# Ten of the odd layer's modulation runs moved from TensorE to GpSimd, beside the even layer's feed-forward

## The chip, the cores and the metric

The kernel runs on one core of a Trainium2 chip. The metric is the device time of one execution in microseconds (us). The core has five engines that run beside each other and meet at semaphores: TensorE (PE, matrix products into the PSUM banks), VectorE (DVE), ScalarE (ACT), GpSimd (POOL, which can't reach PSUM) and SyncE (SP), whose queue issues nearly all DMA loads.

## The reference, cut to what matters

A block with a mixture of experts is followed by two transformer layers over 256 tokens of width 1024. Both are modulated by one vector `c`:

```python
cond = jax.nn.silu(c)                                   # 1 x 1024
for l in range(2):
    mod = cond @ ada_w[l] + ada_b[l]                    # 1 x 6144
    sh1, sc1, g1, sh2, sc2, g2 = split(mod, 6)
    h = rms_norm(x, norm_mix[l]) * (1 + sc1) + sh1
    y = even_mixer(h) if l % 2 == 0 else odd_mixer(h)
    x = x + g1 * (y @ w_out[l])
    h = rms_norm(x, norm_ffn[l]) * (1 + sc2) + sh2
    x = x + g2 * ((silu(h @ wg) * (h @ wu)) @ wd)       # hidden width 2816
```

All data are float32. The change concerns `cond @ ada_w[l]`, a product of one row with a 1024 x 6144 matrix, for each layer 12 pieces of 1024 x 512 (2 MB each).

## The kernel before, in words

The tokens' products are made from weights split in a high and a low part. A load of 2 MB is four chunks of 128 x 1024. For each chunk ScalarE copies the high part (`begin`), VectorE subtracts it from the chunk to leave the low part in place (`ring_r<-ring,W_c_r` or `X_c_r`), and TensorE makes the three products of high and low parts: 24 matmuls of 256 columns, or 12 of 512. `Feed(lag=5)` issues `begin` of a chunk five chunks ahead of its use, and six buffers for the high part bound how far ahead that gets.

Loads go through a ring of `NR = 5` slots of 2 MB, in the order of `plan.loads`. SP issues them in that order; before each it waits until the load that had the slot five loads earlier has been used (`freed`, lines 396 to 402, waited for at line 640). A load that waits holds back all behind it.

A piece of the modulation is a **run** and a **close**. The run (`ada` on TensorE, line 1832) makes 8 matmuls of 512 columns with the weights of the piece into bank 7 (`ps[7]`), which leaves 128 partial rows. ScalarE copies the bank to `acc` (`s_acp`). The close multiplies `acc` with ones: for an ordinary piece four small products, which make columns that VectorE adds to the bias into `modc` (`s_modc`); for the last two pieces of the odd layer (`row_gate`) two products of 512 columns that make a row spread over all partitions, which ScalarE copies to `gates` (`s_gate`). Bank 7 and `acc` exist once, so runs and closes take turns; the next run waits until the bank is read out. `cs` holds silu(c)/32, and `csr` is `cs` repeated 32 times for the run.

The order of work is written by `Plan`: `ada(point)` puts the close of the piece before and a new run at a point of the program. Points are `("u", n, u)`, just after the scores of unit u of attention n; `("f", i)`, at `begin` of chunk i; `("n", l, which)`, inside a modulation (`modulated`), after the squares; and `("o", j)`, ahead of an output projection. Each engine walks the same points. Pieces 0 to 11 are of the even layer and 12 to 23 of the odd one. Pieces 12 and 13 run in the even layer's attention, 14 at the even feed-forward's modulation, 15 in its down projection, 16 at the odd layer's first modulation, and 17 to 23 in the odd attention, one in each second unit up to unit 12.

The stages in which the change works are, in order: output projection of the even mixer, `ffn(0)` (a modulation, 11 loads of gate and up weights, 6 loads of down weights), the odd layer's first modulation, its projections `kvo`, `q0`, `q1`, the odd attention of 16 units (`attend(4, ...)`), output projection, `ffn(1)`. A modulation (`modulated`) adds the gated result to `x` on VectorE, squares on ScalarE, sums on TensorE, makes the reciprocal root on VectorE in eight small operations (`root_parts`, line 1202), spreads it with TensorE, and then gives eight slices of the input in high and low part (`scaled` and `rest`, line 1363). TensorE's products of the next stage wait for these slices.

Side work, like head norms, is stepped between these by `side.go`. GpSimd makes masks and constants at the start and selects in the even layer's index search; after `attend(3, 2)` it has nothing to do.

Of the kernel before, what the change touches and what calls it, by code (L numbers as in the profile page):

```python
# [9 lines left out]
ALU = mybir.AluOpType  # L10
# [10 lines left out]
class Chain:  # L21
# [3 lines left out]
    def __init__(self, e, own):  # L25
        self.e, self.own, self.n, self.last = e, own, {}, None
# [50 lines left out]
class Feed:  # L77
# [30 lines left out]
    def product(self, i0, n, then):  # L108
        self.then[i0 + n - 1] = then
        for i in range(i0, i0 + n):  # L110
            self(i)
# [9 lines left out]
class Plan:  # L121
# [1 line left out]


    def __init__(self):
        self.loads, self.ada_order, self.rows = [], [], {}
        self.chunks, self.first = [], {}
        self.pending = None
        self.moe, self.experts = {}, []
# [13 lines left out]
    def ada(self, point):  # L143
        self.close(point)
        v = self.pending = len(self.ada_order)
        self.ada_order.append((v // 12, v % 12, self.load("ada", v // 12, v % 12)))
        self.rows.setdefault(point, []).append((v, "run"))

    def product(self, name, n, part=None):
        k = self.load("w", name)  # L150
# [19 lines left out]
            if u == wo_at:  # L170
                self.out_loads(j)

    def ffn(self, l, turn_run, run):
        self.first["gu", l] = len(self.chunks)
        for u in range(11):
            k = self.load("gu", l, u)
            for q in (0, 2, 1, 3) if u == 0 else range(4):
                self.feed(k, q)
            if u == 0 and turn_run:
                self.ada(("n", l, 3))  # L180
        self.first["dn", l] = len(self.chunks)
        for u in range(6):
            k = self.load("w", ("dn", l, u))
            for q in range(min(4, 22 - 4 * u)):
                if run is not None and 4 * u + q == run:
                    self.ada(("f", len(self.chunks)))
                if run is not None and 4 * u + q == run + 3:
                    self.close(("f", len(self.chunks)))
                self.feed(k, q)


def make_plan():
    p = Plan()
    for name in ("gqk", "mqk", "mkv"):
        p.product(name, 4)
    for name in ("mvq", "gv", "gr"):
        p.product(name, 4)
    p.units(1, 8, (0, 2, 4, 6), 2, 0)
    p.close(("o", 0))
    p.out_proj(0)  # L200
    for g in range(NX // 4):
        for name in ("w_gate", "w_up", "w_down"):
            for q in range(4):
                p.experts.append(p.load("moe", name, g, q))
    k = p.load("w", "ak")
    p.first["ak"] = len(p.chunks)
    for q in range(3):
        p.feed(k, q)
    p.ada(("n", 0, 0))
    p.feed(k, 3)  # L210
    for name in ("aq", "av", "kvi"):
        p.product(name, 4)
    p.product("tli", 2)
    p.ada(("f", len(p.chunks)))
    p.product("bq", 4)
    p.close(("f", len(p.chunks) - 1))
    p.units(2, 8, (0, 2, 4, 6))
    p.units(3, 8, (0, 2, 4, 6), 2, 1)
    p.close(("o", 1))
    p.out_proj(1)  # L220
    p.ffn(0, True, 6)
    k = p.load("w", "kvo")
    p.first["kvo"] = len(p.chunks)
    for q in range(4):
        p.feed(k, q)
    p.ada(("n", 1, 0))
    p.product("q0", 4)
    p.product("q1", 4)
    p.units(4, 16, (0, 2, 4, 6, 8, 10, 12), 8, 2)
    p.close(("o", 2))  # L230
    p.out_proj(2)
    p.ffn(1, False, None)
    p.end = len(p.chunks)
    return p


def build(nc, A, out_ap, dbg):
    ctx = ExitStack()
    with ctx:
        part = [ctx]  # L240

        def sb(name, shape, dt=FP):
            return part[0].enter_context(nc.sbuf_tensor(name, shape, dt))

        def both(name, shape):
            with nc.sbuf_tensor(name + "_r", shape, FR) as rounded:
                pass
            return sb(name, shape), rounded
# [6 lines left out]
        def sem(name):  # L255
            return ctx.enter_context(nc.semaphore(name))
# [3 lines left out]
        ring, ringR = both("ring", [128, NR, 4096])  # L260
# [19 lines left out]
        modc = sb("modc", [128, 2, 6, 8])  # L280
        gates = sb("gates", [128, 1024])
        cs = sb("cs", [128, 8])
        acc = sb("acc", [128, 512])
        csr = sb("csr", [128, 8, 32])
        qcol = sb("qcol", [128, 18])
# [70 lines left out]
        s_rowx, s_cs, s_ar, s_acp, s_ac, s_gate, s_modc = [sem("s_ada_" + n) for n in ("row_exp", "cs", "run", "copied", "closed", "gate", "col")]  # L356
# [19 lines left out]
        plan = make_plan()  # L376
        nload = len(plan.loads)
        m0, m1_ = plan.experts[0], plan.experts[-1]
        order, slot, before = list(range(NR)), [], {}
# [11 lines left out]
        landed, used = [], [0] * (NR + MR)  # L391
# [4 lines left out]
        freed = {}  # L396
        for i, (k, q) in enumerate(plan.chunks):
            freed[k] = (s_use, i + 1)
        for v, (_, _, k) in enumerate(plan.ada_order):
            freed[k] = (s_ar, v + 1)  # L400
        for m, k in enumerate(plan.experts):
            freed[k] = (s_mm, m + 1)

# [317 lines left out]
        def gpsimd(pool):  # L721
            G = Chain(pool, s_pool)
# [20 lines left out]
            def attend(n, beside):  # L743
                for u in range(len(attns[n].units)):
                    side.go(beside)
                    if n == 3 and u == 4:
                        side.until(ev, "sel1")
# [38 lines left out]
            side.until(ev, "sel0", "bT")  # L786
            attend(3, 2)
            side.end()

# [382 lines left out]
        def vector(dve):  # L1174
# [567 lines left out]
            def ffn(l, n):  # L1742
# [29 lines left out]
                feed.drain()  # L1772

            ffn(0, 1)


# [786 lines left out]
```

## Time and profile before

| what | value |
|---|---|
| device time, median of 3 runs | 1473.1 us (1470.25 to 1476.48) |
| the profiled execution's own time | 1468.73 us |
| its span, first to last instruction | 1467.0 us |
| mean granted clock of TensorE | 0.880 of full speed |
| TensorE, VectorE, ScalarE, GpSimd busy | 1191.2, 615.8, 475.6, 7.6 us |
| read from memory | 366.28 MB, 250 GB/s over the span |

The profile is of one execution. A page gives busy times, the chain of work that ended last and the costliest groups of instructions. Timelines give the start and the length of instructions in us, and in brackets the idle time ahead of one and who ended it. `csr` marks a run, `ones,acc` the close of an ordinary piece, `acc,ones` and `gates,ones` the close of a row piece. All operations of VectorE, ScalarE and GpSimd that go through the helper `Chain` have line L32, all matmuls line L1826 and all transposes line L1830, so tiles tell them apart. The granted clock is given as a part of 2.4 GHz.

### The profile page before, as it was taken

What the parts mean: (1) busy time and instruction counts of PE and PEld (TensorE: products, weight loads), DVE (VectorE), ACT (ScalarE), POOL (GpSimd) and SP (SyncE); (2) the same over time, 40 slices, a digit from 0 to 9 for tenths busy, and PEclk for the clock granted to TensorE, in tenths of its full rate; (3) what the DMA queues carried; (4) which work ended last, traced back from release to release, by engine and by line L of the source; (5) the groups of instructions that cost most, each with busy time, mean ns of one, the idle gap of its engine ahead of it and who ended that gap; (6) DMA issues with size and microseconds to landing.
All of it is one profiled execution on the core that took longest, in us unless ns stands there. A gap on an engine that the chain in (4) does not pass through costs nothing.

```text
span 1467.0 us, 19464 instructions
## 1 busy us (share of the span) xinstructions
PE 1191.2 (81%) x7703; PEld 874.9 (60%) x7703; DVE 615.8 (42%) x1240; ACT 475.6 (32%) x767; POOL 7.6 (1%) x54
## 2 busy tenths in 40 slices
PE   5888888575676756846897888999999978999998
PEld 4665565242332323413675438899898735999986
DVE  3473652010010000101663676655535656565553
ACT  4561621000000000002532335555433447455541
POOL 1000000000000000000000000000000000000000
PEclk9897888798888878978897678899999988999999
DMA  8542149999999999999446431865546472655520
GB/s 294 173 150 80 59 168 424 430 429 430 431 429 428 431 430 428 431 425 401 164 152 244 172 116 58 264 204 203 191 151 223 174 274 70 222 181 187 205 98 29
DMA packets 121729, 368.67 MB, mean 251 GB/s; under 512 B 9842, under 2 KB 56093, under 8 KB 110878
## 3 DMA queue, kind: packets, MB, share of 16 engines
q1 hardware_dynamic: 120556, 367.26, 65.1%
q8 instruction: 64, 1.05, 0.3%
q10 hardware_dynamic: 1074, 0.08, 0.1%
q14 instruction: 35, 0.29, 0.1%
HBM read 366.28 MB, written 1.05 MB: 250 GB/s over the span
## 4 chain that ended last, share of the span: by engine, by line
PE 57%; DMA 22%; DVE 12%; ACT 5%; issue 3%; SPq 1%; DVEq 0%; ACTq 0%
PE ps L1826 54%; DMA more<-in_w_gate_dram 8%; DMA more<-in_w_down_dram 7%; DMA more<-in_w_up_dram 6%; PE ps L1830 3%; DVE st L32 3%; DVE ring_r L32 2%; DVE R_c L32 2%; SPq L669 1%; DVE X_c L32 1%; DVE R_a L32 1%; DVE X_a L32 1%; ACT W_c_r L32 1%; ACT X_c L32 1%; DVE sc L32 1%
## 5 line engine op out<-in xcount | busy, mean ns | idle before, releaser
L1826 PE MATMUL ps<-hT_r,ring_r 128*128 128x256 f32 x864 | 243.7, 282 | 0.0
L1826 PE MATMUL ps<-ring,xg 128*32 128x512 f32 x640 | 140.1, 734 | 126.1 <-DMA more<-in_w_gate_dram 79.3
L1826 PEld LDWEIGHTS ps<-ring,xg 128*32 128x32 f32 x640 | 36.9, 132 | 222.3 <-issue 222.3
L1826 PEld LDWEIGHTS ps<-hT_r,ring_r 128*128 128x128 f32 x864 | 166.0, 192 | 0.0
L32 DVE TENSOR_TENSOR ring_r<-ring,W_c_r 128x1024 fp32r<-128x1024 f32 x94 | 115.2, 1225 | 96.3 <-ACT W_c_r L32 92.4
L1826 PE MATMUL ps<-R_c_r,W_c_r 128*128 128x256 f32 x608 | 152.7, 283 | 0.0
L32 DVE TENSOR_TENSOR ring_r<-ring,X_c_r 128x1024 fp32r<-128x1024 f32 x88 | 107.8, 1225 | 95.2 <-ACT X_c_r L32 92.3
L1826 PE MATMUL ps<-R_c_r,X_c_r 128*128 128x256 f32 x576 | 147.7, 284 | 0.0
L1826 PE MATMUL ps<-more,xg 128*32 128x512 f32 x384 | 134.6, 726 | 0.0
L32 ACT ACTIVATE W_c_r<-ring 128x1024 fp32r<-128x1024 f32 x94 | 99.7, 1060 | 87.3 <-PE ps L1826 83.0
L32 ACT ACTIVATE X_c_r<-ring 128x1024 fp32r<-128x1024 f32 x88 | 93.3, 1061 | 89.6 <-PE ps L1826 84.4
L32 DVE TENSOR_TENSOR x<-x,ps 128x512 f32<-128x512 f32 x36 | 24.8, 688 | 231.3 <-PE ps L1826 231.0
L1826 PE MATMUL ps<-hT_r,X_c_r 128*128 128x256 f32 x416 | 118.3, 284 | 2.9 <-DVE R_c_r L32 2.5
L1826 PE MATMUL ps<-hT_r,W_c_r 128*128 128x256 f32 x416 | 118.6, 285 | 1.9 <-DVE R_c_r L32 1.8
L1826 PEld LDWEIGHTS ps<-R_c_r,W_c_r 128*128 128x128 f32 x608 | 108.8, 190 | 0.0
L1826 PEld LDWEIGHTS ps<-R_c_r,X_c_r 128*128 128x128 f32 x576 | 104.0, 191 | 1.5 <-issue 1.5
L1826 PE MATMUL ps<-ring_r,hT_r 128*128 128x512 f32 (+1 forms) x240 | 94.8, 395 | 0.0
L1826 PEld LDWEIGHTS ps<-hT_r,X_c_r 128*128 128x128 f32 x416 | 78.8, 189 | 4.4 <-issue 3.0
L1826 PEld LDWEIGHTS ps<-hT_r,W_c_r 128*128 128x128 f32 x416 | 79.7, 191 | 2.7 <-DVE R_c_r L32 2.2
L1826 PE MATMUL ps<-ring,csr 128*32 128x512 f32 x384 | 63.6, 794 | 13.1 <-DVE modc L32 12.6
L1826 PE MATMUL ps<-ring,hid 128*32 128x512 f32 x320 | 60.2, 654 | 12.7 <-DMA more<-in_w_down_dram 11.6
L1826 PE MATMUL ps<-sel,hn 128*128 128x128 f32 x256 | 63.1, 410 | 2.1 <-DVE sel L32 2.1
(280 smaller groups left out, 1912.4 us busy)
## 6 DMA issues: line engine op xcount, KB each, us to landing
ring<-in_ada_w_dram SPq DMA_DIRECT2D x24, 2048.0 KB, 8.1
ring<-in_w_gate_dram SPq DMA_DIRECT2D x20, 2048.0 KB, 18.9
ring<-in_w_up_dram SPq DMA_DIRECT2D x20, 2048.0 KB, 20.0
ring<-in_w_down_dram SPq DMA_DIRECT2D x20, 2048.0 KB, 19.4
more<-in_w_gate_dram SPq DMA_DIRECT2D x12, 2048.0 KB, 27.9
more<-in_w_up_dram SPq DMA_DIRECT2D x12, 2048.0 KB, 28.4
more<-in_w_down_dram SPq DMA_DIRECT2D x12, 2048.0 KB, 27.9
ring<-in_ffn_gate_dram SPq DMA_DIRECT2D x22, 1024.0 KB, 5.9
```

What stands on the lines that cost most here:

```text
L32: op(*args, **kw).then_inc(sem, 1)
L669: sp.dma_start(dst, src).then_inc(s_w[slot[k]], 16)
L1826: return pe.matmul(out, lhsT, rhs, start=start, stop=stop, skip_group_check=True)
L1830: return pe.transpose(out, in_, ident[0:n, 0:n])
```

## The change

Pieces 14 to 23 no longer run on TensorE. GpSimd scales each of the 8 weight slices of a piece with its column of `cs32` (silu(c)), in place in the ring's slot, and adds it to `acc`: 8 `tensor_scalar` and 7 `tensor_tensor` instructions of 128 x 512, each waiting for the one before. The last raises `s_acp`, which frees the slot and lets TensorE close the piece as before. Each GpSimd run waits for its load and for the close of the piece before (`s_ac`). The loads stand behind gate-up loads 0, 2, 4, 6, 8 and 10, behind down loads 1 and 3, behind the last down load, and behind `kvo`. A close stands at `begin` of the chunk three before the next pooled load; the eighth at the first chunk of `kvo`, the ninth (first row gate) at the first of `q1`, and the last at unit 0 of the odd attention. In steady state closes are eight chunks apart. No run is left in the odd attention, and the two loads of its output projection come right behind `q1`.

```diff
@@ class Plan @@
+    def pool_run(self, shift=-3):
+        self.close(("f", len(self.chunks) + shift))
+        v = self.pending = len(self.ada_order)
+        self.ada_order.append((v // 12, v % 12, self.load("ada", v // 12, v % 12)))
+        self.pooled.append(v)
...
-    def ffn(self, l, turn_run, run):
+    def ffn(self, l, gate_up_runs=(), down_runs=()):
...
-            if u == 0 and turn_run:
-                self.ada(("n", l, 3))
+            if u in gate_up_runs:
+                self.pool_run()
...
-                if run is not None and 4 * u + q == run:
-                    self.ada(("f", len(self.chunks)))
-                if run is not None and 4 * u + q == run + 3:
-                    self.close(("f", len(self.chunks)))
                 self.feed(k, q)
+            if u in down_runs:
+                self.pool_run()
@@ def make_plan @@
-    p.ffn(0, True, 6)
+    p.ffn(0, (0, 2, 4, 6, 8, 10), (1, 3))
+    p.pool_run(0)
...
-    p.ada(("n", 1, 0))
+    p.pool_run(4)
     p.product("q0", 4)
     p.product("q1", 4)
-    p.units(4, 16, (0, 2, 4, 6, 8, 10, 12), 8, 2)
-    p.close(("o", 2))
+    p.out_loads(2)
+    p.close(("u", 4, 0))
     p.out_proj(2)
-    p.ffn(1, False, None)
+    p.ffn(1)
@@ def build @@
+        cs32 = sb("cs32", [128, 8])
...
-            freed[k] = (s_ar, v + 1)
+            freed[k] = (s_acp if v in plan.pooled else s_ar, v + 1)
@@ def gpsimd, at its end @@
+            pool.wait_ge(s_cs, 1)
+            G(pool.tensor_scalar, cs32[:, :], cs[:, :], 32.0, None, ALU.mult)
+            for v in plan.pooled:
+                k = plan.ada_order[v][2]
+                w = ring[:, slot[k], :].rearrange("p (c n) -> p c n", c=8)
+                pool.wait_ge(*landed[k])
+                pool.wait_ge(s_ac, v)
+                G(pool.tensor_scalar, acc[:, :], w[:, 0, :], cs32[:, 0:1], None, ALU.mult)
+                for c in range(1, 8):
+                    G(pool.tensor_scalar, w[:, c, :], w[:, c, :], cs32[:, c:c + 1], None, ALU.mult)
+                    G(pool.tensor_tensor, acc[:, :], acc[:, :], w[:, c, :], ALU.add, up=s_acp if c == 7 else None)
```

## Rows read from the trace of the kernel before

**Rows 1.** The page: the span, and each engine's busy us, share and instructions.
```profile
span 1467.0 us, 19464 instructions
...
PE 1191.2 (81%) x7703; PEld 874.9 (60%) x7703; DVE 615.8 (42%) x1240; ACT 475.6 (32%) x767; POOL 7.6 (1%) x54
```

**Rows 2.** Windows: stretch, length, busy us of each engine, granted clock, DMA share, GB/s.
```profile
940.00:1055.00 115.00, 115.00 (x979) 115.00 (x978) 67.81 (x73) 59.42 (x73) 0.00 (x0) 1.00 0.61 202
1146.00:1158.00 12.00, 12.00 (x53) 9.76 (x53) 10.35 (x21) 6.37 (x8) 0.00 (x0) 1.00 0.81 291
1172.00:1195.00 23.00, 15.24 (x85) 7.05 (x83) 10.58 (x37) 8.11 (x19) 0.00 (x0) 0.70 0.53 188
1195.00:1207.00 12.00, 12.00 (x106) 6.81 (x105) 8.40 (x34) 8.49 (x25) 0.00 (x0) 1.00 1.02 377
1226.00:1233.00 7.00, 4.31 (x40) 2.50 (x36) 4.35 (x17) 5.87 (x18) 0.00 (x0) 1.00 0.00 0
```

**Rows 3.** The chain in order of time, 920 to 1135 us: start, us, what.
```profile
929.79 125.61 PE ps L1826 x1050
```

**Rows 4.** VectorE's groups by form, 940 to 1055 us.
```profile
L32 DVE TENSOR_TENSOR ring_r<-ring,X_c_r 128x1024 fp32r<-128x1024 f32 x22 | 27.0, 1225 | 19.7 <-ACT X_c_r L32 18.7
...
L32 DVE TENSOR_TENSOR R_c_r<-sc,R_c_r 128x512 fp32r<-128x512 f32 x10 | 6.9, 692 | 1.0
```

**Rows 5.** Timeline of GpSimd: start us, us, line, operation, what it waited for.
```profile
4.16 0.40 POOL L32 TENSOR_SCALAR_AFFINE_SELECT negw<-negd 128x256 f32<-128x256 f32 x1
4.63 0.15 POOL L32 IOTA iotI<- 128x32 int32 x1
...
814.44 0.29 POOL L32 TENSOR_SCALAR_AFFINE_SELECT R_c<-R_c 128x128 f32<-128x128 f32 x1 [709.92 <-DVE R_c L32]
```

**Rows 6.** Timelines of VectorE and TensorE at the first modulation.
```profile
923.90 0.42 DVE L32 SCALAR_TENSOR_TENSOR sc<-st 128x256 f32<-128x256 f32 x1
...
922.22 3.64 PE L1826 MATMUL ps<-ring,csr 128*32 128x512 f32 x16
925.79 1.22 PE L1826 MATMUL ps<-ident,sc 128*128 128x128 f32 x4
```

**Rows 7.** Timeline of TensorE at the start of the even down projection.
```profile
1057.96 0.95 PE L1826 MATMUL ps<-ones,acc 128*128 128x1 f32 x8
1062.29 2.55 PE L1826 MATMUL ps<-ring,csr 128*32 128x512 f32 x16 [3.37 <-DVE modc L32]
```

**Rows 8.** Timeline of TensorE at the odd layer's first modulation.
```profile
1129.83 1.92 PE L1826 MATMUL ps<-ring,csr 128*32 128x512 f32 x16
1131.98 0.71 PE L1826 MATMUL ps<-ident,sc 128*128 128x128 f32 x4 [0.24 <-DVE sc L32]
```

**Rows 9.** Timeline of TensorE at the start of the odd attention.
```profile
1178.87 3.64 PE L1826 MATMUL ps<-ring,csr 128*32 128x512 f32 x16 [5.13 <-DVE modc L32]
...
1189.45 3.64 PE L1826 MATMUL ps<-ring,csr 128*32 128x512 f32 x16
```

**Rows 10.** Timeline of TensorE in the odd attention: two units.
```profile
1195.55 0.49 PE L1826 MATMUL ps<-R_c 64*128 64x128 f32 x4
1195.97 1.92 PE L1826 MATMUL ps<-ring,csr 128*32 128x512 f32 x16
...
1199.19 1.05 PE L1826 MATMUL ps<-ones,acc 128*128 128x1 f32 x8
...
1201.35 0.49 PE L1826 MATMUL ps<-R_c 64*128 64x128 f32 x4
```

**Rows 11.** TensorE's groups by form, 1195 to 1226 us.
```profile
L1826 PE MATMUL ps<-acc,ones 128*128 128x512 f32 x4 | 2.2, 644 | 0.0
L1826 PE MATMUL ps<-gates,ones 1*128 1x512 f32 x4 | 2.2, 640 | 0.0
```

**Rows 12.** Timeline of ScalarE past the last run: the same operation two units apart.
```profile
1227.40 0.51 ACT L32 ACTIVATE X_c<-X_c,s 128x257 f32<-128x257 f32 x1
...
1231.65 0.51 ACT L32 ACTIVATE X_c<-X_c,s 128x257 f32<-128x257 f32 x1
```

More of the change, by code:

```diff
@@ L125, in __init__ @@
     def __init__(self):
-        self.loads, self.ada_order, self.rows = [], [], {}
+        self.loads, self.ada_order, self.rows, self.pooled = [], [], {}, []
         self.chunks, self.first = [], {}
```

## The prediction

> **What bounds the kernel now.** I read the page first, then the windows, then the chain in order of time with the timelines of single stretches. The page [rows 1] shows TensorE busy for 81% of a span of 1467.0 us and GpSimd for 1%; the time around the span is 1.7 us, since the profiled execution took 1468.73 us. The three runs shown have the median 1473.1 us, 4.4 us more: I make the sum against 1468.7 and carry its difference over to 1473.1. The change touches nothing before the even layer's feed-forward, so only 920 to 1240 us matters. The windows [rows 2] show that there TensorE is busy throughout, in the feed-forward (115 of 115 us) and in the odd attention (12 of 12), with VectorE at 59% in the feed-forward and 86% in the odd projections. The chain [rows 3] is TensorE alone for 125.6 us: 1050 matmuls, 0.120 us each, so a chunk of 24 costs 2.87 us. What lengthens TensorE's queue counts in full; what VectorE or ScalarE do counts where TensorE waits for them.
>
> **Part 1: what leaves the odd attention.** Seven runs and seven closes stood in the 16 units. In the steady part two units take 5.80 us (1195.55 to 1201.35), of which the run is 1.92 and the close 1.05 [rows 10]; the last two closes are of the row form and cost 2.2 [rows 11]. Without them TensorE needs 5.80 - 1.92 - 1.05 = 2.8 us for two units, and the next engine sets the pace. That is ScalarE: past the last run it takes 4.25 us for two units, 1227.40 to 1231.65 [rows 12]. Five such pairs, three at 5.8 and two at about 6.9, become 5 x 4.25: 31.3 - 21.3 = 10 us. At the start, the second run waits 5.13 us for VectorE's bank copy and then takes 3.64, and the third takes 3.64 again [rows 9], because the lower level of the clock is granted for much of that stretch (mean 0.70 [rows 2], full being 2.4 GHz and the lower level 1.2). VectorE's head norms stay in that stretch, so of these 12 us I count about 6.5: the second unit's scores need not wait, and the third run stood just before the first turn. Together 16.5 us. Against it: an engine at 2.8 us of work in 4.25 may be granted the lower level, as a run shows it (3.64 against 1.92 [rows 9, 10]); then the pair costs 2.8 x 1.9 = 5.3 rather than 4.25 and the gain is 11. I take 14.
>
> **Part 2: what the even feed-forward gains and loses.** The run in its down half goes: 2.55 us, and with it 3.37 us in which TensorE waited for VectorE to free bank 7 [rows 7]. Five more closes come in (seven rather than two), 0.95 each [rows 7]: 4.75. Net -1.2. They are in front of chunks that TensorE has ready five ahead, so VectorE's copy after each is hidden. The run beside the first modulation (3.64 us) ends at 925.8, and the spreading of the reciprocal root starts only then, while VectorE had it ready at 924.3 [rows 6]: 1.5 us to gain if nothing else is late. The run beside the odd layer's first modulation ended just when VectorE was ready (0.24 us of idle remain [rows 8]): nothing to gain. There a close now stands in front of the squares: +1.0. The close of the first row gate moves into the odd projections, where TensorE has 12.0 of 12 us busy [rows 2]: +2.2 [rows 11]. ScalarE loses ten copies of bank 7, off the chain.
>
> **Part 3: the GpSimd run.** A run is 8 one-input and 7 two-input operations on 128x512, each waiting for the one before. No such row exists. The nearest are the selects: 0.29 us for 128 columns, 0.40 for 256, and 0.47 from one start to the next [rows 5]; 0.11 more per 128 columns gives 0.62 busy and 0.69 start to start at 512. For two inputs the bounds are the same price (0.69) and twice it (1.38); I double the streaming part alone, 0.69 + 0.44 = 1.13. A run is 8 x 0.69 + 7 x 1.13 = 13.4 us, bounds 10.4 and 15.2. The room for it: a run starts when TensorE has closed the one before and must end by the next close, 8 chunks on, 8 x 2.87 = 22.9 us, 23.9 with the close. Alone it fits with 9 us to spare and the whole gain stands. The GPSIMD Engine Reference of the Trainium skill (section 3.1) gives 4497 ns for a two-input add of 2048 columns, an estimate of 1.1 to 1.2 us for 512, so by it the sum stays.
>
> **Part 4: does GpSimd run beside VectorE?** In the trace its selects on real data run only after a wait for VectorE (709.92 us for one [rows 5]), so no row shows both reading. Bounds: full overlap, costing nothing, and no overlap with VectorE's instructions that read two SBUF tensors. Per 8 chunks those are 8 subtractions of 1.225 and 2 of 0.692 [rows 4]: 11.2 us. Full exclusion needs 13.4 + 11.2 = 24.6 us, and about 1.2 for close and semaphores, against 23.9: up to 1.9 us of stall in each of six periods, 11 us. If the 0.25 us of each GpSimd operation that isn't streaming overlaps (15 x 0.25 = 3.8), there is none. I take 5. VectorE's own delays in the feed-forward are covered by its five-chunk lead: it is idle for 47 of 115 us [rows 2]. They are not covered in the two modulations, where TensorE waits for VectorE. Run 22 starts with the close in front of the odd layer's modulation and lasts through it: seven small two-input operations and eight of 0.49 us each can meet a GpSimd operation of 0.6 to 1.05 us. Bounds 0 and 8 us; I take 4. In the first modulation run 14 is well under way (its slot comes free in the middle of the output projection): I put 2.5 us of delay against the 1.5 us gained, +1; bounds -1.5 and +3. In the projections VectorE is at 10.35 of 12 us [rows 2] and run 23 shares it: bounds 0 and 5, I take 2.
> The Trainium skill (SBUF — State Buffer, Who interferes with whom) says that a VectorE instruction with two SBUF inputs and a GpSimd instruction that reads SBUF exclude each other for the whole instruction. By that rule the sum is near the upper ends of these bounds, by plain overlap at the lower ones; no row here decides.
>
> **The queues.** On SP's queue every pooled load keeps its slot until GpSimd's last operation; loads behind it wait in order. The tightest is the gate-up load five loads after a pooled one: its slot comes free at a close, and its chunks are wanted two units (23 us) later. DMA share is 0.61 there [rows 2]; a third load for each two adds about half, under 1. I put nothing on it. If GpSimd is late, TensorE's close waits, and with it all later chunks, VectorE's column copy and GpSimd's next run.
>
> **The sum.** -14 (attention) - 1.2 (closes for the down run) + 1 (first modulation) + 5 (late runs) + 1 + 4 (odd modulation) + 2.2 (row close) + 2 (projections) = 0. So 1468.7 in the profiled execution's terms, **1473 us** beside the median.
>
> **Rivals.**
> *Full overlap, faster.* GpSimd and VectorE don't touch. For it: nothing in the trace speaks against, and VectorE is idle 41% of the feed-forward. Sum: -14 - 1.2 - 1.5 + 1 + 2.2 = -13.5, so 1459.6 us.
> *GpSimd paces the feed-forward, slower.* One mechanism: the run and VectorE's 11.2 us add up beyond the period. It decides from a run over 12.7 us under full exclusion (23.9 - 11.2). At 15.2 a period is 15.2 + 11.2 + 1.2 = 27.6, so 3.7 us of stall, six times: 22 rather than 5. The odd modulation then takes 7 rather than 4 and the projections 5 rather than 2: 1468.7 + 17 + 3 + 3, with the attention at -13, 1492.7; beside the median 1497 us.
> *The clock.* The attention without runs stays at the lower level throughout and hands it to the output projection: its gain is 8 and not 14, 1479 us. Against it: between 1226 and 1233, without runs, where ScalarE sets the pace already, the full level was granted [rows 2].
>
> **How the numbers follow.** My forecast (partial exclusion) has 0.40, full overlap 0.34, GpSimd as the pace 0.20, the clock alone 0.06. The forecast's own range is 1466 to 1481. The range for 8 in 10 leaves out only the outer part of both side cases: 1457 to 1493. Faster by over 0.5% (7.4 us, about what a measurement of this kernel can tell from no change): full overlap nearly whole and a tenth of the forecast, 0.35. Slower: GpSimd's case and a fifth of the forecast, 0.29. Within: 0.36.
>
> **What would show it.** In the new profile: one GpSimd run from first to last operation (13.4 alone, 20 to 24 shared) and whether its operations are longer while VectorE subtracts; TensorE's idle time in front of its ones-by-acc matmuls; VectorE's small operations in the modulation before the odd projections, 0.2 us apart or more; the time for two units (4.25 or 5.3) and the granted clock beside it. The prediction is wrong if GpSimd's operations are far from 0.69 and 1.13, if the two engines overlap wholly, or if the attention has another bound than ScalarE.

## The result, and the profile after

The changed kernel takes 1519.5 us (median of 4 runs, 1514.76 to 1521.33) against 1471.7 for the kernel before on the same chip: ratio 1.0318, interval 1.0278 to 1.0358. It is slower by 3.2%; I had forecast no change, and the time lies far above my range. The profiled execution took 1518.23 us, its span is 1516.5, 49.5 us more than [rows 1].

The page of the changed kernel: the span, busy us of each engine, then tenths of busy time, of the granted clock and of GpSimd in 40 slices.

```profile
span 1516.5 us, 19276 instructions
...
PE 1194.9 (79%) x7543; PEld 894.7 (59%) x7543; DVE 656.6 (43%) x1240; ACT 469.5 (31%) x757; POOL 258.2 (17%) x205
...
PE   5888877566665675667896888888897867999998
...
POOL 1000000000000000000000005899895630000000
PEclk9897888788896897887996578999999787899999
```

TensorE has 160 matmuls less and yet is busy for 1194.9 us, 3.7 more than before; VectorE is busy for 41 us more with as many instructions. Of GpSimd's 258 us, some 250 are in one block; the rest is at the start, as before.

By landmarks in both timelines (first and last product of a stage, first scores) the 49.5 us divide like this:

| stage | before | after | difference |
|---|---|---|---|
| up to the first product of the even feed-forward | 928.8 | 935.8 | +7.0 |
| the even feed-forward, first to last product | 197.6 | 229.5 | +31.9 |
| from there to the first product of `kvo` (odd modulation) | 8.1 | 22.1 | +14.0 |
| projections, to the first scores of the odd attention | 37.8 | 46.8 | +9.0 |
| odd attention, to the first product of its output projection | 67.5 | 54.4 | -13.1 |
| the rest | 227.2 | 227.9 | +0.7 |

**The feed-forward.** Windows of the changed kernel, with the columns of [rows 2]: first the same 115 us as there, then one period from a GpSimd run to the next (950.75 to 980.8), then the last 40 us with a run but without a close in the way, then the odd modulation.

```profile
940.00:1055.00 115.00, 101.54 (x789) 100.99 (x789) 70.33 (x66) 48.03 (x59) 99.24 (x58) 0.91 0.67 220
950.60:980.70 30.10, 24.60 (x201) 24.43 (x202) 21.41 (x19) 14.25 (x18) 26.65 (x15) 0.94 0.85 278
...
1125.70:1166.00 40.30, 40.30 (x344) 40.30 (x343) 13.61 (x11) 12.73 (x12) 25.05 (x15) 1.00 0.75 275
1166.00:1187.00 21.00, 8.31 (x38) 7.87 (x37) 14.41 (x26) 4.18 (x10) 19.62 (x13) 0.56 0.31 113
```

GpSimd is now busy for 99 of 115 us and TensorE for 101.5, with 789 matmuls where it had 979. That period is 30.1 us where I had 23.9; from 950.75 to 1125.8 the six periods are 27.3 to 30.3. Beside a run (1125.7 to 1166) TensorE is as fast as before; only a close that comes too early for GpSimd stops it. The view of TensorE's waits from 935 to 1170 us (us in total, times, the longest), and the timelines of GpSimd and TensorE around one such close:

```profile
PE ps L1846 <- POOL acc L32: 19.9, 6, 5.5
```

```profile
974.91 2.41 POOL L32 TENSOR_SCALAR ring<-ring,cs 128x512 f32<-128x512 f32 x1
977.41 1.26 POOL L32 TENSOR_TENSOR acc<-acc,ring 128x512 f32<-128x512 f32 x1
...
978.81 1.84 PE L1846 MATMUL ps<-ones,acc 128*128 128x1 f32 x8 [5.50 <-POOL acc L32]
980.51 0.56 PE L1846 MATMUL ps<-hT_r,X_c_r 128*128 128x256 f32 x1
980.87 0.41 PE L1846 MATMUL ps<-R_c_r,X_c_r 128*128 128x256 f32 x1
981.09 0.41 PE L1846 MATMUL ps<-hT_r,ring_r 128*128 128x256 f32 x1
```

TensorE waits 5.50 us for the last addition, its close then takes 1.84 us and not 0.95, and the next products have 0.21 us between starts, not 0.12: after the idle time it is granted the lower of its levels, 1.2 in place of 2.4 GHz, for a while (0.89 to 0.94 on average over each of the six periods; 1.00 in 1125.7 to 1166 and in [rows 2]). The waits themselves are 19.9 us; what else the feed-forward lost is products made at this clock, as experiment 1 shows.

**The GpSimd run.** Its first instructions, beside a VectorE that has few subtractions to do, and its groups from 940 to 1120 us, with their means in ns:

```profile
923.08 1.63 POOL L32 TENSOR_SCALAR acc<-ring,cs 128x512 f32<-128x512 f32 x1 [73.70 <-DMA ring<-in_ada_w_dram]
924.80 1.57 POOL L32 TENSOR_SCALAR ring<-ring,cs 128x512 f32<-128x512 f32 x1
926.46 1.27 POOL L32 TENSOR_TENSOR acc<-acc,ring 128x512 f32<-128x512 f32 x1
...
944.91 1.33 POOL L32 TENSOR_TENSOR acc<-acc,ring 128x512 f32<-128x512 f32 x1
```

```profile
L32 POOL TENSOR_SCALAR ring<-ring,cs 128x512 f32<-128x512 f32 x43 | 86.1, 2002 | 4.2
L32 POOL TENSOR_TENSOR acc<-acc,ring 128x512 f32<-128x512 f32 x43 | 62.6, 1456 | 3.6
```

The first run takes 23.2 us (923.08 to 946.24); those in full feed-forward 26 to 28. A scaling is 1.56 us alone and 1.65 from start to start, where I had 0.62 and 0.69; an addition is 1.27 and 1.37, where I had 1.13 from start to start. VectorE's groups over the same stretch as [rows 4]:

```profile
L32 DVE TENSOR_TENSOR ring_r<-ring,X_c_r 128x1024 fp32r<-128x1024 f32 x16 | 24.3, 1518 | 10.6 <-ACT X_c_r L32 9.6
L32 DVE TENSOR_TENSOR R_c_r<-sc,R_c_r 128x512 fp32r<-128x512 f32 x7 | 9.2, 1314 | 0.7
```

1225 and 692 ns have become 1518 and 1314, and GpSimd's operations are longer too: each side waits for the other.

**The odd modulation.** Timelines of VectorE and TensorE from the close of piece 21, at 1165:

```profile
1166.17 0.16 DVE L32 TENSOR_TENSOR modc<-ps,cols 128x4 f32<-128x4 f32 x1 [7.65 <-PE ps L1846]
1166.44 1.62 DVE L32 TENSOR_TENSOR ring_r<-ring,X_c_r 128x1024 fp32r<-128x1024 f32 x1
1168.16 1.55 DVE L32 TENSOR_TENSOR ring_r<-ring,W_c_r 128x1024 fp32r<-128x1024 f32 x1
1169.82 2.12 DVE L32 TENSOR_TENSOR ring_r<-ring,X_c_r 128x1024 fp32r<-128x1024 f32 x1
...
1172.82 2.11 DVE L32 SCALAR_TENSOR_TENSOR x<-ps,modc,x 128x256 f32<-128x256 f32 x4
```

```profile
1165.18 0.95 PE L1846 MATMUL ps<-ones,acc 128*128 128x1 f32 x8
1173.90 6.96 PE L1846 MATMUL ps<-ones,sc 128*128 128x1 f32 x32 [7.76 <-ACT sc L32]
1184.28 1.22 PE L1846 MATMUL ps<-ident,sc 128*128 128x128 f32 x4 [3.43 <-DVE sc L32]
1187.43 0.77 PE L1846 MATMUL ps<-X_c_r,hT_r 128*128 128x512 f32 x1 [1.93 <-DVE R_c_r L32]
```

The close stands at the first chunk of `kvo`, and in VectorE's queue its `modc` addition is ahead of three subtractions, which were done before the feed-forward's end in the kernel before, and of the gated additions to `x`. VectorE idles 7.65 us for a close that TensorE can make only after its last product. Then three subtractions, and only then `x`; ScalarE's squares and TensorE's sums wait, the clock falls, and the sums take 6.96 us, not the 3.63 of the kernel before:

```profile
1126.27 3.63 PE L1826 MATMUL ps<-ones,sc 128*128 128x1 f32 x32
```

GpSimd's timeline beside the first and the third of these subtractions shows how the two engines meet:

```profile
1166.30 1.56 POOL L32 TENSOR_SCALAR acc<-ring,cs 128x512 f32<-128x512 f32 x1 [14.14 <-issue]
...
1169.60 1.26 POOL L32 TENSOR_TENSOR acc<-acc,ring 128x512 f32<-128x512 f32 x1
```

The third subtraction starts inside the addition, which ends at 1170.86, and ends 1.08 us after it: of its 1.23 us nearly all comes behind the addition. The first starts 0.14 us into the scaling, which ends at 1167.86, and ends only 0.20 us after it: it got through while the scaling still ran. So it is all through this trace: the 15 subtractions that start inside an addition, before its last 0.1 us, end 1.07 to 1.09 us after it; the 11 that start 0.14 to 0.35 us into a scaling of 1.56 us end 0.19 to 0.21 us after it. An operation of GpSimd that starts inside a subtraction is done 1.43 to 1.46 us (scaling) or 1.14 to 1.16 us (addition) after the subtraction's end, so it waits for all of it.

**The odd attention.** TensorE's timeline, first and last scores of six pairs of units without runs:

```profile
1247.11 0.80 PE L1846 MATMUL ps<-R_c 64*128 64x128 f32 x4
...
1274.91 0.49 PE L1846 MATMUL ps<-R_c 64*128 64x128 f32 x4
```

27.8 us for six pairs, 4.6 each, against 5.80 [rows 10]: between the 4.25 that I took and the 5.3 of the lower clock, and the granted clock from 1247 to 1286 is 0.74. In these 39 us TensorE is busy for 31.4, VectorE for 30.1 and ScalarE for 27.3; TensorE's waits there end on VectorE (5.6 us, 7 times) and once on ScalarE (1.0).

### The profile page after: what moved, and what is told of

It is laid out like the page before. It is cut to its first block and busy times, and to the rows that moved or that the text cites. A ratio compares the mean times of both kernels' runs of the same rounds, so it can differ in the third digit from the quotient of the medians.

```text
span 1516.5 us, 19276 instructions
## 1 busy us (share of the span) xinstructions
PE 1194.9 (79%) x7543; PEld 894.7 (59%) x7543; DVE 656.6 (43%) x1240; ACT 469.5 (31%) x757; POOL 258.2 (17%) x205
## 5 line engine op out<-in xcount | busy, mean ns | idle before, releaser
L1846 PE MATMUL ps<-hT_r,ring_r 128*128 128x256 f32 x864 | 250.8, 290 | 0.0
L1846 PEld LDWEIGHTS ps<-hT_r,ring_r 128*128 128x128 f32 x864 | 169.5, 196 | 0.0
L32 DVE TENSOR_TENSOR ring_r<-ring,W_c_r 128x1024 fp32r<-128x1024 f32 x94 | 125.9, 1340 | 98.0 <-ACT W_c_r L32 93.6
L32 DVE TENSOR_TENSOR ring_r<-ring,X_c_r 128x1024 fp32r<-128x1024 f32 x88 | 119.4, 1357 | 88.5 <-ACT X_c_r L32 85.0
L32 POOL TENSOR_SCALAR ring<-ring,cs 128x512 f32<-128x512 f32 x70 | 133.6, 1909 | 6.8
L1846 PE MATMUL ps<-hT_r,W_c_r 128*128 128x256 f32 x416 | 122.0, 293 | 2.4 <-DVE R_c_r L32 2.3
L1846 PEld LDWEIGHTS ps<-R_c_r,W_c_r 128*128 128x128 f32 x608 | 114.5, 200 | 0.0
L32 POOL TENSOR_TENSOR acc<-acc,ring 128x512 f32<-128x512 f32 x70 | 99.0, 1414 | 5.8
```

The lines of the kernel that those rows point to most:

```text
L32: op(*args, **kw).then_inc(sem, 1)
L1846: return pe.matmul(out, lhsT, rhs, start=start, stop=stop, skip_group_check=True)
```

## The experiments

Each kernel is timed against the kernel before on its chip. The changed kernel has 1.0318.

### 1. GpSimd's work taken away, its places kept

The changed kernel, in which a run is one operation of 8 columns. It leaves out scaling and adding.

```diff
-                G(pool.tensor_scalar, acc[:, :], w[:, 0, :], cs32[:, 0:1], None, ALU.mult)
-                for c in range(1, 8): ...
+                G(pool.tensor_scalar, acc[:, 0:8], w[:, 0, 0:8], cs32[:, 0:1], None, ALU.mult, up=s_acp)
```

> Leaves out the scaling and the summing: each of GpSimd's ten runs is one operation on 128x8, so the modulation of the odd layer's pieces is not computed; the order of loads, waits and closes is that of the changed kernel. Theory A (GpSimd's run is too long, and everything lost beyond that follows from it): all stalls vanish and what is left is the gain forecast for full overlap, 13.5 us below the kernel before, ratio 0.991, with the odd modulation as short as before (8 us from the last product to the first). Theory B (part of the loss is in the order, because VectorE waits for the close at the first chunk of kvo before it may add the feed-forward's result): the odd modulation stays 7 to 10 us longer than before even without GpSimd's work, ratio 0.995 to 0.998.

Measured: 1472.99 us, ratio 1.0013 (0.9988 to 1.0038), above what either theory gave, though the modulation is as theory B has it. So 3.05% of the 3.2%, 45 us, is GpSimd's work. By stages: the feed-forward is 195.1 us (after: 229.5, 34 less), the attention keeps its gain (54.8), but the odd modulation takes 18.6 us, 10.5 more than before, without any GpSimd work. The windows of the feed-forward, first the changed kernel, then this one:

```profile
935.80:1165.30 229.50, 209.32 (x1642) 207.99 (x1643) 130.41 (x116) 89.76 (x106) 191.36 (x112) 0.92 0.67 229
934.70:1129.80 195.10, 195.07 (x1643) 195.10 (x1643) 101.46 (x116) 89.93 (x106) 2.16 (x7) 0.99 0.78 270
```

For the same matmuls TensorE is busy 14 us longer in the changed kernel, at a mean granted clock of 0.92 and not 0.99; with the 19.9 us of waits that is the whole difference. The timelines of the odd modulation, VectorE then TensorE:

```profile
1130.60 0.16 DVE L32 TENSOR_TENSOR modc<-ps,cols 128x4 f32<-128x4 f32 x1 [7.74 <-PE ps L1843]
1130.87 1.23 DVE L32 TENSOR_TENSOR ring_r<-ring,X_c_r 128x1024 fp32r<-128x1024 f32 x1
```

```profile
1136.34 6.96 PE L1843 MATMUL ps<-ones,sc 128*128 128x1 f32 x32 [5.78 <-ACT sc L32]
```

The wait of 7.7 us is the same. The modulation's loss is mostly one of order; the 3.5 us from 18.6 to 22.1, in which the subtractions' lengthening is (1.23 to 1.6 and 2.1), are GpSimd's.

### 2. The last ordinary close three chunks earlier

```diff
-    p.pool_run(0)
+    p.pool_run()
```

> The changed kernel with only the close of piece 21 moved, from the first chunk of kvo to three chunks earlier, in the even down projection. Theory B: VectorE no longer waits there, the odd modulation becomes 8 to 12 us shorter, ratio to the kernel before about 1.025 against 1.032. Theory A: GpSimd's contention makes that modulation long, so the time stays within 3 us of 1519.5.

Measured: 1519.5 us, 1.0330 (1.0309 to 1.0350). The modulation falls from 22.1 to 13.1 us, as the order of VectorE's queue asks, but the feed-forward rises from 229.5 to 243.6. The view of TensorE's waits:

```profile
PE ps L1846 <- POOL acc L32: 28.6, 7, 9.4
```

A seventh close has become late, by 9.4 us, since only six chunks lie between it and the one before. What is won in one place is paid in the other, because GpSimd has no time to give. Theory B was right on the modulation and missed the time, for which I had put 1.025.

### 3. The same close at the last chunk of the feed-forward

```diff
-    p.pool_run(0)
+    p.pool_run(-1)
```

> The changed kernel with the close of piece 21 one chunk ahead of the first chunk of kvo, at the last chunk of the feed-forward, eight chunks after the close before. GpSimd's runs and their contention stay. If VectorE's wait for that close costs what the kernel without GpSimd's work showed (10.5 us in the odd modulation), and the late run costs no more there than at the other closes (3 to 5 us), the ratio goes from 1.032 to about 1.027. Rival: the stall only moves into the feed-forward, as with the earlier place, ratio 1.032.

Measured: 1509.57 us, 1.0278 (1.0260 to 1.0296). The modulation takes 10.3 us, the sums of squares 4.67 us right behind the last product; the feed-forward 237.9. One chunk's difference in place is worth 12 us in the modulation and costs 8 in the feed-forward; by the ratio it is worth 6 us, near the 1.027 that I expected.

### 4. A constant in place of the column

The changed kernel scales with 0.5, so the modulation's values are other ones.

```diff
-                    G(pool.tensor_scalar, w[:, c, :], w[:, c, :], cs32[:, c:c + 1], None, ALU.mult)
+                    G(pool.tensor_scalar, w[:, c, :], w[:, c, :], 0.5, None, ALU.mult)
```

> The changed kernel with the constant 0.5 in place of the column of silu(c) in GpSimd's scaling, so the modulation of the odd layer is wrong. If the column operand is what makes a scaling 1.56 us rather than the 0.62 that I had worked out from the selects, the scaling falls to 0.6 to 0.8 us, a run to 15 us alone, and the ratio to 1.01 or below. If the scaling costs 1.56 us whatever its scalar is, nothing changes: 1.032.

Measured: 1507.16 us, 1.0254 (1.0236 to 1.0272). The fastest scaling is 1.49 us, 0.07 less than with the column, and in the feed-forward:

```profile
L32 POOL TENSOR_SCALAR ring<-ring 128x512 f32<-128x512 f32 x42 | 79.2, 1886 | 3.6
```

Fetching the operand is not what makes the scaling dear. A scaling is 0.12 us shorter here (1886 for 2002), 0.9 for a run, and over six periods that is 5.6; the feed-forward takes 223.2 us in place of 229.5. So a shorter run makes a shorter feed-forward, which the rival, the same price whatever the scalar, left out. By the ratio the kernel gained 9.4 us; 4.6 of what the profile has lie before the feed-forward, where the two kernels are alike.

### 5. The scaling as an operation with two inputs

```diff
-                    G(pool.tensor_scalar, w[:, c, :], w[:, c, :], cs32[:, c:c + 1], None, ALU.mult)
+                    G(pool.tensor_tensor, w[:, c, :], w[:, c, :], cs32[:, c:c + 1].to_broadcast([128, 512]), ALU.mult)
```

> The changed kernel, but GpSimd scales a slice by a two-input multiplication with the column spread over 512, in place of the operation with a scalar operand. Theory A (GpSimd's own price paces the even feed-forward, and its operation with a scalar costs more than one with two inputs): the scaling takes 1.27 us in place of 1.56, a run is 8 x 0.29 = 2.3 us shorter, so up to six stalls shrink by up to 2.3 us each: ratio 1.023 to 1.028 in place of 1.032. Rival (the price is that of a pass over 128 x 512 whatever the form, or two-input operations collide more with VectorE's): the run does not get shorter and the ratio stays at 1.032 or above.

Measured: 1516.59 us, 1.0305 (1.0278 to 1.0332), not told apart from the changed kernel and above my 1.023 to 1.028. GpSimd's groups from 940 to 1120 us, and a multiplication of its first run:

```profile
L32 POOL TENSOR_TENSOR acc<-acc,ring 128x512 f32<-128x512 f32 x44 | 77.5, 1761 | 3.5
L32 POOL TENSOR_TENSOR ring<-ring,cs 128x512 f32<-128x512 f32 x44 | 65.4, 1486 | 3.4
...
L32 POOL TENSOR_TENSOR acc<-ring,cs 128x512 f32<-128x512 f32 x7 | 8.7, 1242 | 23.6 <-issue 23.6
```

```profile
926.03 1.04 POOL L32 TENSOR_TENSOR ring<-ring,cs 128x512 f32<-128x512 f32 x1
```

The multiplication did get cheaper (1.04 us for 1.56 in the first run, 1486 ns for 2002 beside VectorE), but the additions became dearer (1761 for 1456). The first run takes 18.7 us (924.92 to 943.62), which is under the room of 22.9; those in the feed-forward take 23.4 to 27.2, and four closes still wait, for 12.9 us in all. So with this price it is contention that makes the runs late. That fits what the subtractions showed: a scaling lets one through while it runs, and an operation with two inputs does not. In the profile the feed-forward takes 216.8 us rather than 229.5, and 11.3 of the 12.7 us are lost again: 5.6 before it begins, 1.9 in the modulation and 3.8 in the projections. The first of these lies where both kernels are alike, and I can't explain it. So the price of the form is shown, its worth for the whole is not.

### 6. The same work in the kernel before, with nobody waiting

The kernel before plus ten times the 15 GpSimd operations, on memory that is not in use there. No close, no slot and no load hangs on them, so only contention is left.

```diff
+            for n, at_use in enumerate([first["gu", 0] - 4 + 8 * k for k in range(8)] + [first["kvo"], first["q1"] - 4]):
+                pool.wait_ge(s_use, at_use)
...
+                for c in range(1, 8):
+                    G(pool.tensor_scalar, g1, g0, cs[:, c:c + 1], None, ALU.mult)
+                    G(pool.tensor_tensor, g2, g2, g1, ALU.add)
```

> The kernel before, with the same ten sequences of 15 GpSimd operations beside the even feed-forward and the odd projections, on idle memory, triggered by TensorE's progress, and nobody waiting for them before the odd feed-forward. It shows what the contention alone costs. Theory A with contention as in the traces (GpSimd's operations 0.8 to 1 us longer where VectorE's subtractions meet them): VectorE's subtractions lengthen but the five chunks of lead cover them; the two modulations and the projections lose 8 to 15 us together, ratio 1.005 to 1.010. Rival, no contention that matters: 1.000 to 1.002. Rival, contention is the main cost and the waits for late runs come second: 1.02.

Measured: 1482.0 us, 1.0078 (1.0059 to 1.0097): 11.5 us for contention alone. In the profile the feed-forward takes 0.7 us more, the odd modulation 2.3, the projections 8.3; 1.3 more lie before the feed-forward and 1.4 in the attention. VectorE in the feed-forward (940 to 1055), and the windows of the projections in this kernel and in the one before:

```profile
L32 DVE TENSOR_TENSOR ring_r<-ring,W_c_r 128x1024 fp32r<-128x1024 f32 x22 | 35.7, 1622 | 15.8 <-ACT W_c_r L32 14.5
```

```profile
1139.00:1185.00 46.00, 39.25 (x162) 31.32 (x161) 37.90 (x54) 16.47 (x22) 43.56 (x27) 0.89 0.39 138
```

```profile
1134.50:1172.30 37.80, 37.02 (x162) 29.71 (x162) 27.38 (x54) 16.43 (x22) 0.00 (x0) 0.95 0.47 169
```

In the feed-forward subtractions are 1622 ns long (1454 those that write beside `X_c_r`) and cost next to nothing, since VectorE is five chunks ahead. In the projections the same 54 instructions take VectorE 37.9 us and not 27.4, and 8 of those 10.5 us end up in the time.

### 7. Only the new tile

The kernel before with `cs32` declared and not used: 32 bytes of each partition, by which all tiles behind move; and a second kernel with a tile of 64 bytes in the same place.

```diff
+        cs32 = sb("cs32", [128, 8])
```

> The kernel before with nothing but the 128x8 tile cs32 declared, which moves the tiles behind it by 32 bytes a partition. The changed kernel was 7 us behind already at the even feed-forward's first product, before GpSimd's work. If the tile's place does that: ratio 1.004. If it is the spread of single executions: 0.998 to 1.002.

> The kernel before with one unused tile of 64 bytes a partition declared where the change declares one of 32. If what costs 0.4% is that the tiles behind leave a multiple of 64 bytes, this one costs nothing: ratio 0.999 to 1.001. Rival: any move of the tiles costs, by 0.4% again or by another amount: 1.003 or more.

Measured: 32 bytes 1475.41 us, 1.0044 (1.0016 to 1.0073); 64 bytes 1476.92 us, 1.0043 (1.0027 to 1.0058). A move of the tiles costs 0.4% either way, about 6 us, so it isn't that they leave a multiple of 64 bytes. In both profiled executions the odd modulation takes 11.0 us, not 8.1, because TensorE makes its run there (`csr`) at the lower clock, in 3.64 us and not 1.92. That alone doesn't mark the tile: the kernel of experiment 10, which has no new tile, needs 3.53 us for the same run and 9.4 for the modulation.

### 8. The changed kernel with its scales in an old tile

```diff
-        cs32 = sb("cs32", [128, 8])
+        cs32 = st[:, 240:248]
```

> The changed kernel with its scales in unused columns of an existing tile, so that no tile moves; nothing else differs. If the 7.0 us which the changed kernel has lost before the feed-forward come from the tiles' places, the ratio falls from 1.032 to about 1.027 and the first product of the even feed-forward starts near 928.8 in place of 935.8. Rival (the 7 us come from the order of the loads or from the program itself): it stays at 1.032 and the product at 935.

Measured: 1511.61 us, 1.0283 (1.0266 to 1.0301), 0.35% less than the changed kernel. That is what the tile alone would give, but the two intervals overlap, so this experiment by itself doesn't show it. The first product of the feed-forward starts at 934.2, not at the 928.8 that I expected; the profiled execution was the slowest of its four (1517.66 us), so its stages don't show where the difference lies.

### 9. ScalarE scales, GpSimd only adds

ScalarE, which in the feed-forward is busy for half the time, scales the slices in place, two at each chunk; GpSimd makes 7 additions in a run. Eight pieces are pooled (14 to 21). Their closes stand three chunks later than in the changed kernel, eight chunks apart as there, and that of the last at the feed-forward's last chunk, five after the one before, and the two row pieces go back to TensorE, at units 5 and 8 of the odd attention. The second kernel of this experiment has the scales in the old tile too.

```diff
+                for v, c in plan.scales.get(i, ()):
...
+                    copy(z, z, scale=cs32[:, c:c + 1], up=s_slopes)
@@ GpSimd's run
-                G(pool.tensor_scalar, acc[:, :], w[:, 0, :], cs32[:, 0:1], None, ALU.mult)
-                    G(pool.tensor_scalar, w[:, c, :], w[:, c, :], cs32[:, c:c + 1], None, ALU.mult)
```

> ScalarE scales the slices, two at each of four chunks (0.6 us each), GpSimd only adds (7 operations, 9.6 us alone, 12 to 14 beside VectorE), pieces 14 to 21 only, the close of 21 at the last chunk of the feed-forward, pieces 22 and 23 on TensorE at units 5 and 8 of the odd attention. If the length of GpSimd's run and the close at kvo were what cost, no close waits for GpSimd, the odd modulation is near 8 us, the attention some 9 us shorter than before: ratio 0.994 to 0.997. If contention or the five more closes eat that: 1.000. If ScalarE becomes late for TensorE's chunks: above 1.005.

> The kernel in which ScalarE scales and GpSimd only adds, with the eight scales in unused columns of an existing tile, so that no tile behind it moves. If the tile's place costs what it costs alone in the kernel before (ratio 1.0044) whatever else runs, this gives 0.9997 - 0.0044 = 0.995, faster than the kernel before by 0.5%. Rival: the place costs only in the stages where the kernel before is bound as it is, and this version hides it or loses it again: 0.998 to 1.000.

Measured: 1468.55 us, 0.9997 (0.9983 to 1.0011); with the scales in the old tile 1464.01 us, 0.9965 (0.9952 to 0.9977). The first misses my 0.994 to 0.997, and the second lies between my 0.995 and the rival's 0.998. The second is the only kernel here that is faster than the kernel before, by 5 us, and its interval lies apart from the first's. Its GpSimd group and TensorE's waits in the feed-forward, and the windows of the feed-forward and most of the attention:

```profile
L32 POOL TENSOR_TENSOR acc<-acc,ring 128x512 f32<-128x512 f32 x48 | 84.3, 1755 | 7.0 <-ACT ring L32 0.3
```

```profile
PE ps L1853 <- POOL acc L32: 2.0, 1, 2.0
```

```profile
928.50:1129.50 201.00, 199.01 (x1650) 198.83 (x1651) 130.43 (x128) 132.18 (x174) 94.79 (x56) 0.98 0.76 261
1181.00:1230.00 49.00, 39.02 (x232) 20.09 (x232) 34.81 (x131) 29.77 (x90) 0.00 (x0) 0.73 0.35 109
```

Without the scalings a GpSimd run takes 12.3 to 13.9 us; one close is late, by 2.0 us, though its additions are as long as ever beside VectorE (1755 ns for 1270 alone). TensorE is busy for 199 of 201 us. The attention takes 58.9 us against 67.5: two of seven runs there cost about 4 of the 13 us. Since the closes moved with it, this kernel doesn't show the length of the run by itself.

### 10. The kernel before with its runs spread otherwise

No GpSimd: in the odd attention the seven runs stand at units 3, 5, 7, 9, 11, 13 and 14, not at its start, the loads of the output projection at unit 11 and not 8, and the close of piece 14 three chunks before the down run.

```diff
-    p.units(4, 16, (0, 2, 4, 6, 8, 10, 12), 8, 2)
+    p.units(4, 16, (3, 5, 7, 9, 11, 13, 14), 11, 2)
```

> The kernel before, nothing on GpSimd: the seven runs of the odd attention moved from units 0, 2, ... 12 to 3, 5, 7, 9, 11, 13, 14, the loads of the output projection to unit 11, and in the down projection the close of piece 14 three chunks ahead of the run of 15. If the gain of the attention without runs (12.7 us) lay mostly in its start, where the second run waits 5.13 us for the copy of bank 7 and two runs are at the lower clock, some 6 us of it come back this way and 3 us in the down projection: ratio 0.994. If it lay evenly over the units: 0.998 to 1.000.

Measured: 1467.7 us, 0.9999 (0.9981 to 1.0017), no difference. The profiled execution (span 1462.5) is the fastest of its ten and doesn't speak for the median; in it the attention takes 66.5 us against 67.5. So in the attention it is the runs' own time that costs, not where they stand: moving them out is what can gain. In the same profile the feed-forward is 4.9 us shorter, since TensorE no longer waits there for bank 7 (3.37 us [rows 7]); the medians don't show that gain either.

## Why the prediction was wrong

**The step that failed is part 3, the price of the GpSimd run.** I priced the one-input operation from selects of up to 256 columns, 0.69 us from start to start, and let the upper bound double only the operations with two inputs. It is 1.65 (1.56 busy; with a constant 1.49), and the two-input addition 1.37 against my 1.13. A run nearly alone is 23.2 us, not 13.4, and far above my upper bound of 15.2; I had scaled another kind of operation from a range that ends at half the size. The room of 22.9 us is filled by the run alone. The outcome is that of the rival *GpSimd paces the feed-forward*, at its place and with a larger size: six late closes, 19.9 us of waits. Its sum is not: it puts all of VectorE's 11.2 us on top of the run, which with 23.2 us would make a period of 35.6, and the periods are 27.3 to 30.3. Beside VectorE a run is only 2.8 to 5.0 us longer; the rest is its own price. Experiment 1 shows that this is GpSimd's work (34 us in the feed-forward); experiments 4 and 9 agree that a shorter run makes a shorter feed-forward. Neither I nor the rival counted what the idle time does to the clock: some 14 of the 34 us (34.4 less 19.9; TensorE is busy for 209.3 and not 195.1 us with the same matmuls). I had 5 for late runs and -1.2 for the closes, so +4 for the stage; the trace has +32.

**Missed: VectorE's queue in the odd modulation.** I wrote that a close in front of the squares costs +1.0, TensorE's time alone. I followed what is queued behind a wait on SP and on TensorE and not on VectorE: three subtractions and the additions to `x` stand behind the close's column copy. It costs 10.5 us against the kernel before (experiment 1), 7.6 against the one with the tile alone (11.0, experiment 7); experiments 2 and 3 move it and get 9 and 12 back.

**Part 4, contention.** That the two engines exclude each other in part was right: subtractions grow from 1225 to 1518 ns, an addition from 1.27 to up to 2.4 us, and of VectorE's 11.2 us 2.8 to 5.0 come on top of a run. It is not 0.25 us of each operation that overlaps, as I supposed: a subtraction overlaps with the end of an addition by some 0.15 us (1.23 less 1.08) and with a scaling that came first by some 1.0 (1.23 less 0.20). By the rule of the Trainium skill (SBUF — State Buffer, Who interferes with whom), which I gave in the prediction, the exclusion lasts for the whole instruction. The trace agrees for the additions (subtractions end 1.07 to 1.09 us after them) and for a GpSimd operation that comes second; it doesn't for a scaling that comes first, 0.20 us after whose end a subtraction is done. There the measurement decides. The odd modulation got 3.5 us of it (22.1 less 18.6; 2.3 in experiment 6) for my 4. The projections got 5.9 (46.8 less 40.9) to 8.3 for my 2, above my bound of 5: VectorE was busy for 10.35 of 12 us there [rows 2]. In the feed-forward VectorE's own delays were hidden, as I said: 0.7 us in experiment 6.

**Part 1, the attention.** -14 forecast, -13.1 measured, -12.7 in experiment 1. Of the gain 10.4 us (27.8 against 38.2) lie in the six pairs from unit 2 to unit 14, and 3.4 ahead of them. That the size came out is in part luck: I had ScalarE as the bound at 4.25 us, and it is busy for 27.3 of 39 us while TensorE's waits end mostly on VectorE. *The clock* as a rival fell: a pair takes 4.6 us and not 5.3, at a granted clock between the levels.

**Part 2.** The closes for the down run: I had -1.2, experiment 1 shows -2.5 in the feed-forward. The row close in the projections: +2.2 forecast, and the projections take 40.9 us in experiment 1 for 37.8, +3. Both are right within 1.3 us.

**The start.** "The change touches nothing before the even layer's feed-forward" failed: 7 us were lost there. GpSimd's last select, [rows 5] at 814.44, now starts at 820.08. Experiment 7 and the two kernels of experiment 9 show that the tile declared for the scales, which moves others, costs 5 to 6 us of the whole, and experiment 8 agrees within its noise. A good part of it seems to lie in this start: over all the profiled executions the feed-forward's first product stands at 928.4 to 930.1 in the four kernels without a new tile, at 931.2 to 941.4 in the nine with one, and at 934.2 in experiment 8. Why is open.

**Together.** Against the ratio: GpSimd's work 3.05% (pace and clock in the feed-forward 34 us, contention in modulation and projections 9), the tile 0.4%; the order without either is left at -0.3%. By the stages of the profiled executions it is 13 us won in the attention less 10.5 in the modulation and 3 in the projections, with 2.5 won in the feed-forward. The full-overlap rival is out by the lengthened operations alone.

**Open:** why the tile's place costs its 0.4%, why experiment 5 starts the feed-forward 5.6 us later, and how the 34 us of the feed-forward divide between the run's price and contention where both are as large as here. A scaling and addition in a single GpSimd operation was not measured.

## What to carry to other kernels

Work is free on an idle engine only if its length, with the contention, is below the distance to the point where somebody waits for it. An operation that no row shows must be measured at its own shape before such a plan is made; a price scaled from another kind of operation was off by a factor of 2.4 (1.65 for 0.69 us). When a wait moves, read the order of each engine that takes part in it, VectorE's too: a column copy of 0.16 us ahead of three subtractions cost 10.5 us. And a late close costs TensorE the wait and then, at the lower clock, some three quarters as much again.

## What the runs showed of the hardware

- GpSimd's `tensor_scalar` on 128x512 float32 takes 1.56 us with a column and 1.49 with a constant, more than its two-input `tensor_tensor` (1.27 for an addition, 1.04 for a multiplication with a column spread over 512; experiment 5).
- Ten times 15 such operations beside VectorE cost 0.8% with nobody waiting for them; VectorE's two-input subtraction of 1024 columns grows from 1.225 to 1.45 and 1.62 us on average (two groups).
- VectorE's two-input subtraction that starts inside a GpSimd addition ends 1.07 to 1.09 us after it, so it waits for the whole; one that starts early in a 1.56 us `tensor_scalar` ends 0.20 us after it. A GpSimd operation that starts inside a subtraction waits for its end.
- For 19.9 us of waits in six pieces TensorE was busy another 14 us at the lower clock (experiment 1).
- An unused tile of 32 or 64 bytes a partition made the whole kernel 0.4% slower (1.0016 to 1.0073, 1.0027 to 1.0058).
